# The gated unit's layer-norm scale and bias moved from the token rows to behind the spatial product, in a two-layer trunk on one core

## What is computed

```
def sgu_mixer(h, w_in, ln_g, ln_b, w_s, b_s, w_out):
    z = gelu(h @ w_in);  u, v = split(z, 2, axis=-1)
    v = layernorm(v, ln_g, ln_b)                 # (v - mean) * rsqrt(var + eps) * ln_g + ln_b
    v = v.reshape(B, nblk, 128, 4, 256)          # blocks of 128 tokens, 4 groups of 256 channels
    ws = where(sgu_mask()[None], w_s, 0)         # w_s: (4, 128, 128)
    s = einsum('gpq,bnqgc->bnpgc', ws, v) + b_s.T[None, None, :, :, None]
    return (u * s.reshape(B, S, 1024)) @ w_out
```

## Time and profile before

| | before |
|---|---|
| median of 3 runs | 1216.95 us (1216.09 to 1217.52) |
| the profiled execution's own time | 1217.14 us |
| its span, first to last instruction | 1215.3 us |
| PE busy in the span | 1197.4 us (99%) |
| PE weight loads | 996.5 us (82%) |
| DVE busy | 661.8 us (54%) |
| ACT busy | 398.4 us (33%) |
| POOL busy | 177.1 us (15%) |
| mean granted TensorE clock | 0.994 |

### The profile page before, as it was taken

How to read it: one execution, slowest core, us unless ns; L and a number is a source line. 1 busy time by engine, 2 the same in 40 slices (tenths; PEclk the granted TensorE clock), 3 DMA queues, 4 the chain that set the end, 5 groups by cost and what they waited for, 6 DMA issues and landing times.

```text
span 1215.3 us, 14873 instructions
## 1 busy us (share of the span) xinstructions
PE 1197.4 (99%) x5538; PEld 996.5 (82%) x5538; DVE 661.8 (54%) x872; ACT 398.4 (33%) x538; POOL 177.1 (15%) x103
## 2 busy tenths in 40 slices
PE   9999999999999999999999999999999999999995
PEld 7888888888888888888888888888888888888884
DVE  7786565534534535564587565566542643534533
ACT  7655333322222212223444433343321321222210
POOL 0040053000000000160343061016000000000041
PEclk9999999999999999999999999999999999999997
DMA  9432123322222232333234422112223232232311
GB/s 372 162 117 75 35 87 121 120 89 104 97 93 98 92 104 87 104 117 126 70 105 139 156 88 100 56 39 102 92 98 104 86 104 89 101 104 86 104 36 69
DMA packets 34749, 125.34 MB, mean 103 GB/s; under 512 B 3984, under 2 KB 4112, under 8 KB 34064
## 3 DMA queue, kind: packets, MB, share of 16 engines
q1 hardware_dynamic: 33552, 121.65, 29.5%
q10 hardware_dynamic: 1152, 3.06, 0.8%
HBM read 122.59 MB, written 2.10 MB: 103 GB/s over the span
## 4 chain that ended last, share of the span: by engine, by line
PE 94%; DVE 3%; ACT 1%; POOL 0%; DMA 0%; issue 0%; DVEq 0%; ACTq 0%; POOLq 0%
PE ps L1040 29%; PE ps L1041 29%; PE ps L1042 29%; PE ps L1088 1%; PE ps L1090 1%; PE ps L1089 1%; PE ps L1229 1%; PE ps L1108 1%; DVE w_lo L669 0%; POOL sq L1029 0%; DVE out_tiles L982 0%; DMA gains<-in_gains 0%; DVE b_lo L676 0%; PE ps L1102 0%; ACT probs L559 0%
## 5 line engine op out<-in xcount | busy, mean ns | idle before, releaser
L1040 PE MATMUL ps<-a_lo,w_hi 128*128 128x512 f32 x704 | 276.4, 393 | 0.0
L441 ACT ACTIVATE w_hi<-w_raw 128x1024 fp32r<-128x1024 f32 x186 | 195.4, 1053 | 242.0 <-PE ps L1042 220.7
L1042 PE MATMUL ps<-a_hi,w_lo 128*128 128x512 f32 x704 | 274.1, 389 | 0.0
L1040 PE MATMUL ps<-b_lo,w_hi 128*128 128x512 f32 x704 | 274.0, 389 | 0.0
L1041 PE MATMUL ps<-a_hi,w_hi 128*128 128x512 f32 x704 | 274.0, 389 | 0.0
L1042 PE MATMUL ps<-b_hi,w_lo 128*128 128x512 f32 x704 | 273.9, 389 | 0.0
L1041 PE MATMUL ps<-b_hi,w_hi 128*128 128x512 f32 x704 | 273.9, 389 | 0.0
L666 DVE TENSOR_TENSOR w_lo<-w_raw,w_hi 128x1024 fp32r<-128x1024 f32 x186 | 231.6, 1247 | 21.9 <-ACT w_hi L441 21.8
L896 DVE TENSOR_TENSOR x<-ps,x 128x512 f32<-128x512 f32 x64 | 44.3, 691 | 213.5 <-PE ps L1042 195.4
L1040 PEld LDWEIGHTS ps<-a_lo,w_hi 128*128 128x128 f32 x704 | 132.2, 188 | 28.1 <-issue 1.0
L1041 PEld LDWEIGHTS ps<-a_hi,w_hi 128*128 128x128 f32 x704 | 132.2, 188 | 27.9 <-issue 1.0
(11 more groups left out here) (147 smaller groups left out, 1173.6 us busy)
## 6 DMA issues: line engine op xcount, KB each, us to landing
w_raw<-in_weights SPq DMA_DIRECT2D x218, 512.0 KB, 3.2
x<-in_x_t SPq DMA_DIRECT2D x2, 1024.0 KB, 7.8
x_tok<-in_x_rows SPq DMA_DIRECT2D x2, 1024.0 KB, 7.7
out_t<-out_tiles SPq DMA_DIRECT2D x8, 256.0 KB, 2.1
mem_raw<-in_mem_t ACTq DMA_DIRECT2D x1, 1024.0 KB, 4.8
mem_raw<-in_mem_t SPq DMA_DIRECT2D x2, 256.0 KB, 5.2
mem_raw<-in_mem_t SPq DMA_DIRECT2D x1, 512.0 KB, 6.5
ln_gain<-in_ln_g ACTq DMA_DIRECT2D x1, 512.0 KB, 3.8
```

The lines of the kernel that those rows point to most:

```text
L441: act.activation(w_hi[:, slot, :], w_raw[:, slot, :], ACT.Copy, scale=row_gain(c) if b is None else 1.0).then_inc(whi_ready, 1)
L1040: pe.matmul(out_ap, s_hi, m_lo, start=start, stop=False)
L1042: return pe.matmul(out_ap, s_lo, m_hi, start=False, stop=stop)
```

## The change

`ln_g` and `ln_b` join the table of per-channel gains (80 to 96 columns); their two 512 KB broadcasts and POOL's eight instructions go away. ACT splits `v_raw` as soon as DVE has normalized it. Behind su tile 2 PE makes one fp32 matmul, `ones` by `ws_raw` (masked), which puts the row sums on all partitions; DVE copies them out, and behind its last su turn it builds `sp_bias` with eight instructions of 128x128. The instruction that takes an sp tile from PSUM now multiplies by `ln_g` and adds `sp_bias`.

```diff
@@ Numbers.walk
         for m in range(8):
             self.add(("su", m), "bank", "ready", "z")
             self.used[self.chunk["su"] + m] = self.ready["su", m]
+            if m == 2:
+                self.add("ws_sums", "bank", "ready")
@@ scalar
-            act.dma_start(ln_gain[:], lng_d.partition_broadcast(P)).then_inc(sgu_loaded, 16)
-            act.dma_start(ln_bias[:], lnb_d.partition_broadcast(P)).then_inc(sgu_loaded, 16)
...
                 if 3 <= m < 7:
-                    act.wait_ge(affine_step, 2 * (m - 3) + 2)
+                    act.wait_ge(norm_ready, m - 2)
                     hi(g_hi[:, m - 3, :], v_raw[:, m - 3, :])
@@ vector
+                if m == 2:
+                    dve.wait_ge(psum_ready, N.ready["ws_sums"] + 1)
+                    dve.tensor_copy(ws_rows[:].rearrange("p g n -> p (g n)"), bank("ws_sums")).then_inc(taken, 1)
                 lo_weights(C["su"] + m + AHEAD)
                 if 3 <= m < 7:
                     lo(N.hi["v_norm", m - 3], g_lo[:, m - 3, :], v_raw[:, m - 3, :], g_hi[:, m - 3, :]).then_inc(lo_ready, 1)
+            for m in range(8):
+                dve.scalar_tensor_tensor(out=sp_bias[:, m, :], in0=ws_rows[:, m // 2, :], scalar=gain("ln_b", m),
+                                         in1=bs[:, m // 2, :], op0=ALU.mult, op1=ALU.add).then_inc(bias_ready, 1)
...
                 dve.wait_ge(psum_ready, N.ready[key] + 1)
-                dve.tensor_tensor(z[:, N.z[key] % 2, :].rearrange("p (b n) -> p b n", b=ST),
-                                  bank(key)[:].rearrange("p (b n) -> p b n", b=ST),
-                                  bs[:, m // 2, None, :].broadcast_to([P, ST, P]),
-                                  ALU.add).then_inc(taken, 1)
+                dve.wait_ge(bias_ready, m + 1)
+                dve.scalar_tensor_tensor(out=z[:, N.z[key] % 2, :].rearrange("p (b n) -> p b n", b=ST),
+                                         in0=bank(key)[:].rearrange("p (b n) -> p b n", b=ST), scalar=gain("ln_g", m),
+                                         in1=sp_bias[:, m, None, :].broadcast_to([P, ST, P]),
+                                         op0=ALU.mult, op1=ALU.add).then_inc(taken, 1)
@@ gpsimd
-            pool.wait_ge(sgu_loaded, 64)
-            for t in range(ST):
-                pool.wait_ge(norm_ready, t + 1)
-                pool.tensor_tensor(v_raw[:, t, :], v_raw[:, t, :], ln_gain[:], ALU.mult).then_inc(affine_step, 1)
-                pool.wait_ge(affine_step, 2 * t + 1)
-                pool.tensor_tensor(v_raw[:, t, :], v_raw[:, t, :], ln_bias[:], ALU.add).then_inc(affine_step, 1)
@@ tensor
             for m in range(8):
                 tile_of(C["su"] + m, ("su", m), a_hi, a_lo)
+                if m == 2:
+                    wait_split(("ws", 0))
+                    wait_bank("ws_sums")
+                    pe.matmul(bank("ws_sums"), ones[:], ws_raw[:].rearrange("p g n -> p (g n)"), start=True, stop=True)\
+                        .then_inc(psum_ready, 1)
```

More of the change, by code:

```diff
@@ L49 @@
 BAND = P + PAD
-GAINS = ("mix0", "mix1", "mem0", "mem1", "kv0", "kv1", "ffn0", "ffn1", "final", "pool_scale")
+GAINS = ("mix0", "mix1", "mem0", "mem1", "kv0", "kv1", "ffn0", "ffn1", "final", "pool_scale", "ln_g", "ln_b")
 PARTS = (("k0", 8), ("v0", 4), ("pool", 2), ("v0b", 4), ("q0", 8), ("o0", 8), ("f0", 64),
@@ L214, in attention_and_mlp, with trunk_kernel @@
             self.tiles("xg_sgu", KT, "hi", "lo")
-def trunk_kernel(nc, x_t, x_rows, mem_t, weights, gains_d, ws_t, bs_d, lng_d, lnb_d, ident_d, band_d, out):
+def trunk_kernel(nc, x_t, x_rows, mem_t, weights, gains_d, ws_t, bs_d, ident_d, band_d, out):
     C = chunk_bases()
@@ L265, in trunk_kernel @@
     pt_hi, pt_lo = at(p_off + 8 * KB, "pt_hi", [P, NT, S], F32R), at(p_off + 12 * KB, "pt_lo", [P, NT, S], F32R)
-    ln_gain, ln_bias = at(p_off, "ln_gain", [P, D]), at(p_off + 4 * KB, "ln_bias", [P, D])
+    ws_rows, sp_bias = at(p_off, "ws_rows", [P, GROUPS, P]), at(p_off + 2 * KB, "sp_bias", [P, KT, P])
     ws_raw = at(p_off + 8 * KB, "ws_raw", [P, GROUPS, P])
@@ L351, in trunk_kernel @@
     norm_ready = sem("norm_ready")
-    affine_step = sem("affine_step")
+    bias_ready = sem("bias_ready")
     gated_ready = sem("gated_ready")
@@ L929, in _ @@
             dve.wait_ge(ln_step, ST + 1)
-            dve.wait_ge(sgu_loaded, 64)
+            dve.wait_ge(sgu_loaded, 32)
             dve.memset(ws_raw[P // 2:P, :, 0:P // 2], 0.0).then_inc(masked, 1)
@@ L1407 @@
              "kv0": norm_memkv_g[0], "kv1": norm_memkv_g[1], "ffn0": norm_ffn_g[0], "ffn1": norm_ffn_g[1],
-             "final": final_norm_g, "pool_scale": pool_scale[0]}
+             "final": final_norm_g, "pool_scale": pool_scale[0], "ln_g": sgu_ln_g[0], "ln_b": sgu_ln_b[0]}
     gains = np.concatenate([np.asarray(gains[g]).reshape(KT, P) for g in GAINS])
@@ L1413 @@
         "bs": np.ascontiguousarray(np.asarray(sgu_b_s)[0]),
-        "ln_g": np.ascontiguousarray(np.asarray(sgu_ln_g)[0]), "ln_b": np.ascontiguousarray(np.asarray(sgu_ln_b)[0]),
         "ident": np.eye(P, dtype=np.float32), "band": band_table(),
```

## The result

The changed kernel takes **1219.67 us** (median of 14 runs, 1218.98 to 1220.67) against 1216.95 us of the kernel before (1216.09 to 1217.78, 14 runs): 2.72 us more, a ratio of 1.0023 with a 95% interval from 1.0015 to 1.0031. The profiled execution took 1220.27 us, its span is 1218.5 us.

A forecast was written before the change was run, and what follows sets the result against it. The chain through DVE, POOL and ACT, not PE, was taken to set k1+5's start. Matmul 0.9 plus chain 1.87 (1.54 + 0.33) gave 2.8 us (2.4 to 3.7), so 1219.7 us from 1216.95; range 1219.3 less 0.9 to 1221.0.

The forecast's parts named there:

- What bounds the kernel: From 631.39 to 656.05 us a chain through DVE, POOL and ACT sets k1+5's start, 0.5 us longer than PE's work.
- The row sums: One fp32 matmul of ones by 512 columns added on PE, which has no idle time there: +0.9 us, paid whole.
- The copy and its wait: DVE's 0.69 us copy, queued ahead of one w_lo and taking su tile 3, costs nothing: DVE waits for PE anyway.
- POOL's part: Removing POOL's 24.0 us of scale and bias is worth nothing, since DVE was waiting for PE at 631.39 us anyway.
- The block: Eight 128x128 sp_bias instructions on DVE ahead of mem_lo, about 0.255 us each, 2.05 us together; upper bound 2.7.
- rival A: Short DVE instructions cost 0.21 us each, so the eight take 1.7 us; time 1219.3 us; chance 0.20.
- The delay behind it: mem_lo and z of sp tile 0 begin 1.54 us later (1.2 to 2.2), after 0.51 us hidden waiting for mem_hi.
- The longer z: DVE's sp z with a gain takes 0.746 against 0.676 us, five times on the chain: +0.33 us (zero to 0.56).
- Where PE waits: PE's idle time spreads over k1+0 (0.5 us), k1+4 (1.2) and k1+5 (0.8), together 2.4 where 0.5 stood.
- B: DVE's waits for ACT in the sp loop absorb the delay, leaving only the matmul: 1217.9 us; chance 0.12.
- C: POOL's leaving speeds DVE up and that reaches PE, the 0.5 us stall vanishing: 1217.3 us; chance 0.04.
- D: PE's waits bring its clock down, one stretch of ten us at 1.2 GHz: about 1230 us; chance 0.04.

The follow-up runs named there:

- the step that shortens the chain: DVE's z of sp tile 0 moved ahead of mem_lo, alone on the kernel before: 1216.47 us against 1216.77, ratio 0.9996.

## Why the prediction was right

- **What bounds the kernel.** The chain through DVE, POOL and ACT behind the last su tile, and not PE, sets when k1+5 starts. Shown: the block added to the kernel before comes out at PE whole, 1.56 us, and the step that shortens the chain takes PE's wait away.
- **The row sums**, 0.9 us: 0.90 between the two su tiles around it. Right, as the row of the same form had it.
- **The copy and its wait**: free, as said. DVE waited 2.96 us for PE ahead of su tile 2 and 3.20 us ahead of su tile 3.
- **POOL's part**: worth nothing, right, and shown alone (-0.09 us, interval 0.9992 to 1.0010, the distance to k1+5 the same to the hundredth). The larger gains table, put at zero, can't be seen beside the scatter of the program's start.
- **The block**: 2.05 us predicted, 2.11 measured; 0.264 us each where I took 0.255. The upper bound, 0.34, is what one shows by itself (0.344), the lower, 0.22, belongs to another kind. The figure of the Trainium skill's "Vector Engine (DVE) Microarchitecture Reference", section 5.2, 75 ns beside the columns, gives 1.67 us for eight, as an estimate; the rows say 0.13 us beside the columns for this kind with a scalar from SBUF, so rival A falls.
- **The delay behind it**: 1.54 us predicted, 1.57 measured at the first sp `z`.
- **The longer z**: 0.33 predicted, 0.29 by the kernel that undoes it; 0.740 us each.
- **Where PE waits**: 0.5, 1.2 and 0.8 us predicted for k1+0, k1+4, k1+5; 0.47, 1.13 and 0.59 measured. Together 2.2 and not 2.4. Most of the rest is that the matmul next after the first one behind a wait comes 0.34 us behind it at 645.50 and 0.31 at 655.58, and not 0.227, which I had counted nowhere.
- **The rivals**: B (absorbed) falls with the block on the kernel before, C (POOL) with POOL's part taken out, D with the granted clock, which is 1.00 from the start to 1200 us in the changed kernel.
- **The bounds**: looser in the working than they should be. The sum's lower bound of 2.4 us takes `z` at its full 0.33; with the zero that stands as its bound it is 2.1. And 1221.0 lies above 1216.95 + 3.7 = 1220.65, so the upper end was widened for scatter. The measured 1219.67 us is near neither end.
- **How near it was**: the parts are shown, 0.90 + 1.83 us against 0.9 + 1.87. That the median came within 0.03 us of 1219.7 is luck: the interval of the ratio is 1 us wide either way. The sum lay 0.3 us over the bound of 0.2%, and so does the measured 2.72 us. The interval, 1.0015 to 1.0031, holds that bound; slower by more than 0.2% is more likely than not, but not shown. The ratio is above 1 beyond doubt.

## What to carry to other kernels

Work taken from an engine ahead of a wait for PE was worth nothing here (24 us of POOL), and new work on an engine in the chain was paid in full once the wait ahead of it was used up: ask of a rewrite not how much it removes, but in front of which wait each new instruction stands. Eight small instructions cost 1.5 us in one place and nothing in the turns just ahead of it, where the same engine waited for PE. And where a stage has a second chain of about PE's length, give each of the two its own sum; here PE had no slack up to the sp tiles, and the chain beside it ended 0.5 us too late.

## What I had not expected

**The end of the program scatters with PE's clock.** The last sums over the channels are eight fp32 pairs in the stretch from 1198 us, which shows a mean granted clock of 0.56 of full speed in the earlier trace rows, and 0.55 in the same work after, from 1201 us; PE had gone idle just ahead of them, waiting for DVE and ACT. In the kernel before (first row) the first three pairs take 0.36 us and the last four 0.56; in the kernel before with `z` of tile 0 first (second row) all eight take 0.36 us:

```profile
1200.24 0.56 PE L1350 MATMUL ps<-ones,ssq 128*128 128x1 f32 x2
```

```profile
1199.27 0.36 PE L1359 MATMUL ps<-ones,sq 128*128 128x1 f32 x2
```

In the first the granted clock is 1.00 from 1199.0 to 1199.8 us and 0.52 from there to 1202.0; in the second it is 1.00 from 1198.5 to 1200.5, through all eight pairs. ACT waits 3.08 us for these sums in the first and 2.10 in the second, and from 2.10 to 3.39 us over all the profiles here, by how many of them run before the clock falls from its upper level (2.4 GHz) to the lower (1.2 GHz). That is up to 1.3 us between executions of like programs, half of what this change costs, and the reason to read small steps from distances in the trace. The start scatters too: DVE's first `k_lo` (L676) comes at 37.91 to 38.60 us in the four kernels that have the code of before up to there, and at 38.22 in the changed one.

**DVE beside POOL.** A 128x1024 instruction of DVE with two tensors in SBUF takes 1.2 to 1.3 us alone and 2.3 beside one of POOL's products (653.13 in the changed kernel, 1.29 at 651.74 in the kernel where POOL is done by then), while the `z`, which reads one tensor from PSUM, keeps its 0.74 us. This agrees with the Trainium skill ("GPSIMD Engine Reference", section 8, Key points), which names instructions with two SBUF inputs as those that contend.

The traces show more: such an instruction, started while POOL's product runs, ends about as long behind the product as its own work takes, as if it did that work only then. POOL's last two products in the changed kernel:

```profile
652.68 1.67 POOL L1030 TENSOR_TENSOR sq<-z,u 128x512 f32<-128x512 f32 x1 [1.29 <-DVE z L962]
656.17 1.66 POOL L1030 TENSOR_TENSOR sq<-z,u 128x512 f32<-128x512 f32 x1 [1.82 <-DVE z L962]
```

They end at 654.35 and 657.83 us. The two `w_lo` that start 0.45 us behind their starts, at 653.13 and 656.62, end at 655.43 and 658.92, 1.08 and 1.09 us behind their ends. In the kernel before it is 1.08 us for both, and for the 128x512 `b_lo` at 643.86 us 0.55. So on this chain the length of POOL's product counts, and not only the work of DVE. Of `mem_lo` behind the early `z` the first half took 1.22 us and the second 2.31, ending 1.08 us behind POOL's product (636.90): that is the 1.1 us that `mem_lo` took longer, and one reason why the early product was worth less than its 2.4 us.

An instruction with one tensor in SBUF was stretched too: the four normalizations (L941) took 0.81 to 2.71 us before, beside POOL's scale and bias, and 0.80 to 0.81 us after.
